# A hybrid decoder step on one core: the finish of a head pair is dealt out over all but the last four steps of the next pair's preparation

## The reference

```
for l in range(DEPTH):
    x = layer_norm(DN_ALPHA * x + 0.5 * swiglu(x, ffn1_w_in[l], ffn1_w_out[l]), ln1_g[l], ln1_b[l])
    proj = x @ w_in[l]
    f_r, f_s, f_g = jnp.split(proj, [R_PROJ, R_PROJ + S_PROJ], axis=-1)
    y_r, ... = rwkv7_mixer(f_r, ...)       # 4 heads x 64
    y_s, ... = swa_prompt(q, k, v, ...)    # window attention
    y_g, ... = gdn_mixer(f_g, ...)         # 4 heads x 64, chunked gated delta rule
    mix = jnp.concatenate([y_r, y_s, y_g], axis=-1) @ w_out[l]
    x = layer_norm(DN_ALPHA * x + mix, ln2_g[l], ln2_b[l])
    x = layer_norm(DN_ALPHA * x + 0.5 * swiglu(x, ffn2_w_in[l], ffn2_w_out[l]), ln3_g[l], ln3_b[l])
```

## Time and profile before

| | |
|---|---|
| median of 3 runs | 3004.49 us (2995.5 to 3006.26) |
| the profiled execution | 3005.59 us, of it the span from first to last instruction 3003.8 us |
| TensorE busy in matmuls | 2742.8 us, 91% of the span |
| TensorE busy in weight loads | 2561.6 us, 85% |
| VectorE busy | 1669.7 us, 56% |
| ScalarE busy | 949.2 us, 32% |
| chain that ended last | TensorE 78%, VectorE 10%, issue 5%, ScalarE 4% |
| mean granted TensorE clock | 0.901 of full speed |

### The profile page before, as it was taken

How to read it: one execution, slowest core, us unless ns; L and a number is a source line. 1 busy time by engine, 2 the same in 40 slices (tenths; PEclk the granted TensorE clock), 3 DMA queues, 4 the chain that set the end, 5 groups by cost and what they waited for, 6 DMA issues and landing times.

```text
span 3003.8 us, 59208 instructions
## 1 busy us (share of the span) xinstructions
PE 2742.8 (91%) x23222; PEld 2561.6 (85%) x23222; DVE 1669.7 (56%) x2503; ACT 949.2 (32%) x1694; POOL 161.5 (5%) x168
## 2 busy tenths in 40 slices
PE   8999999978796989999999999998887778999997
PEld 8999998866675889999999999987765668999996
DVE  5666347745545466664366653566445553666534
ACT  4333233322212243332233332344212222433323
POOL 1030110000000010001100001000000000100011
PEclk9999999976766999999999999998766768999998
DMA  4852234100000323232223222431000012222221
GB/s 110 101 93 86 85 107 121 44 27 1 9 9 1 91 66 90 85 89 83 86 78 88 87 85 85 129 90 41 7 1 8 9 28 86 77 84 84 87 87 59
DMA packets 380501, 201.67 MB, mean 67 GB/s; under 512 B 41461, under 2 KB 376821, under 8 KB 379528
## 3 DMA queue, kind: packets, MB, share of 16 engines
q1 hardware_dynamic: 377928, 197.46, 22.8%
q0 software_dynamic: 2400, 1.82, 1.9%
HBM read 188.07 MB, written 13.34 MB: 67 GB/s over the span
## 4 chain that ended last, share of the span: by engine, by line
PE 78%; DVE 10%; issue 5%; ACT 4%; DMA 1%; SPq 1%; DVEq 0%; POOLq 0%; ACTq 0%; POOL 0%
PE ps L682 51%; PE ps L737 25%; DVE ar L1918 3%; DVE ar L1912 2%; ACT ar L1415 2%; DVE wl L1796 1%; ACT wh L1346 1%; SPq L529 1%; PE ps L1011 1%; DVE x L1912 1%; DMA raws<-in_ffn_w_in 0%; DVE xl L1903 0%; DVE ar L1948 0%; ACT xh L1415 0%; DMA raws<-in_w_in 0%
## 5 line engine op out<-in xcount | busy, mean ns | idle before, releaser
L1796 DVE TENSOR_TENSOR wl<-raws,wh 128x1024 fp32r<-128x1024 f32 x336 | 411.3, 1225 | 673.1 <-ACT wh L1346 668.7
L737 PE MATMUL ps<-ar 64*64 64x64 f32 (+13 forms) x5408 | 517.6, 292 | 146.3 <-ACT ar L1415 39.0
L682 PE MATMUL ps<-xh,wh 128*128 128x272 f32 x2880 | 604.8, 291 | 17.7 <-DVE wl L1796 15.2
L737 PEld LDWEIGHTS ps<-ar 64*64 64x64 f32 (+6 forms) x5408 | 388.7, 177 | 250.2 <-issue 71.8
L682 PE MATMUL ps<-xh,wl 128*128 128x272 f32 x2880 | 599.7, 290 | 0.0
L682 PE MATMUL ps<-xl,wh 128*128 128x272 f32 x2880 | 598.3, 289 | 0.0
L1346 ACT ACTIVATE wh<-raws 128x1024 fp32r<-128x1024 f32 x336 | 354.7, 1057 | 416.6 <-PE ps L682 376.6
L682 PEld LDWEIGHTS ps<-xh,wh 128*128 128x128 f32 x2880 | 457.6, 190 | 21.4 <-DVE wl L1796 17.9
L682 PEld LDWEIGHTS ps<-xl,wh 128*128 128x128 f32 x2880 | 457.8, 190 | 0.0
L682 PEld LDWEIGHTS ps<-xh,wl 128*128 128x128 f32 x2880 | 457.3, 190 | 0.0
L682 PE MATMUL ps<-hh,wh 128*128 128x272 f32 x1408 | 292.3, 289 | 0.0
(11 more groups left out here) (188 smaller groups left out, 2749.9 us busy)
## 6 DMA issues: line engine op xcount, KB each, us to landing
raws<-in_ffn_w_in SPq DMA_DIRECT2D x176, 512.0 KB, 3.7
raws<-in_ffn_w_out SPq DMA_DIRECT2D x64, 512.0 KB, 4.0
raws<-in_w_in SPq DMA_DIRECT2D x42, 512.0 KB, 3.7
raws<-in_ffn_w_out SPq DMA_DIRECT2D x32, 384.0 KB, 3.4
raws<-in_w_out SPq DMA_DIRECT2D x16, 448.0 KB, 4.0
x_kept<-x SPq DMA_DIRECT2D x2, 2176.0 KB, 10.1
x<-x_kept SPq DMA_DIRECT2D x2, 2176.0 KB, 7.9
ar<-in_consts SPq DMA_DIRECT2D x2, 1337.5 KB, 6.7
```

The lines of the kernel that those rows point to most:

```text
L682: ins = pe.matmul(ps[:, bank + h, 0:n1 - h * NH], w[u % 2][:, k, :], a[:, k0 + k, h * NH:n1], start=(first and k == 0 and n == 0), stop=(l ...
L737: return pe.matmul(dst, lhsT, rhs, start=start, stop=stop, **kw)
L1796: dve.tensor_tensor(wl[u % 2][:, :, :], raw[u % 2][:, :, :], wh[u % 2][:, :, :].bitcast(F32), ALU.subtract).then_inc(sem("wl_done"), 1)
```

## The change

A fifth argument of `alternate`, `left`, is the number of steps at the end of the first generator beside which no step of the second stands. The keys of the second are multiplied by (n_first - left) / n_first. In the three rounds `left` is 4; the other two calls keep 0. Every instruction of before is there, with its waits; only the order changes, on each engine alike.

```diff
+NORM_AHEAD = 4
...
-def alternate(first, n_first, second, n_second):
+def alternate(first, n_first, second, n_second, left=0):

-    order = sorted([((k + 1) / n_first, 0) for k in range(n_first)] + [((k + 1) / n_second, 1) for k in range(n_second)])
+    share = (n_first - left) / n_first
+    order = sorted([((k + 1) / n_first, 0) for k in range(n_first)] + [((k + 1) / n_second * share, 1) for k in range(n_second)])
...
     for q in range(3):
-        alternate(prepare(q + 1), PREPARE_STEPS[q + 1], finish(q), FINISH_STEPS)
+        alternate(prepare(q + 1), PREPARE_STEPS[q + 1], finish(q), FINISH_STEPS, NORM_AHEAD)
```

## The result

The changed kernel took 3050.98 us in the median (3047.52 to 3060.32, 4 runs) beside 3005.38 for the kernel before (2995.5 to 3008.21): a ratio of 1.0163, with a 95% interval from 1.013 to 1.0195. The forecast was 3017, the top of the range 3038. The profiled execution took 3049.99 us, its span 3048.2, which is 44.4 more than before.

The account below looks back on a forecast made before the run. TensorE is at nine tenths outside the mixers, so only the rounds can change. Ends -13.6, stalls +16.0, front +4.9 and start -1.6 give +5.7 us a layer, +11.4 for both: from 3005.6 to 3017.0, range 2994 to 3038.

Parts of the forecast that it names:

- The ends: Ends of the three rounds: TensorE's two waits for `ge` (5.3 us each) and 3.0 into the mix saved; -13.6 a layer.
- The inner stalls: Inside the inverses: masks wait for newton (1.9 us) and F22 (3.4, gated pair 2.6), F20 0.45; +16.0 a layer.
- The start of the inverse in round 0: Before round 0's inverse: products of F15 and F16 move into TensorE's 3.83 us wait for VectorE; -1.6 us a layer.
- The clock for the norm: Half clock in inner stalls against faster first products of rounds 1 and 2: even, 0; ends -5 and +8 a layer.
- The front: Front of rounds 1 and 2: F6 before P8 makes VectorE wait, +2.7 and +2.2 us; +4.9 a layer.
- Clearly slower: Rival: the clock falls in four to six inner stalls a layer, 2.2 us each; 3025 to 3033, say 3030; 25%.
- Even: Rival: the rounds are bound by TensorE's total work, delays are absorbed and stalls take what the ends give; 3005; 21%.
- faster: Rival: end gaps close, clock holds over first products, inner stalls half covered, front free; -12.2 us a layer, 2981; 14%.
- The watch on the granted clock: Sign: the sum is wrong if the rounds' granted clock, 0.64 in round 1, moves by more than 0.03.

Follow-up runs that it names:

- The early `ge`: Kernel before, order kept; VectorE only makes the gates' copy `ge` for the next pair ahead of F22 instead of behind it: 2981.71 us, ratio 0.9947.
- F6 put back: Changed kernel with recurrence step F6 back behind P8 in rounds 1 and 2: 3046.01 us, ratio 1.0156 to the kernel before.
- The norm alone: Kernel before with only F19 to F22 moved ahead, not quite to the change's places; F1 to F18 as before: 3012.69 us, ratio 1.0037.
- the front alone: Kernel before with F1 to F18 where the change puts them and F19 to F22 as before: 3032.93 us, ratio 1.0103.
- the fillers: Changed kernel plus products leaving no result, three ahead of B of level 4, four ahead of level 5, all rounds: 3025.48 us, ratio 1.0085.
- the control: Kernel before with the same extra products at the same places, where TensorE doesn't wait: 3018.87 us, ratio 1.0044.
- recurrence-only kernel: Kernel before with only F1 to F12 where the change puts them, F13 to F22 as before: 3025.10 us, ratio 1.0078.

## Why the prediction was wrong

*The ends, -13.6.* Right: 5.3 at `ge` (5.85 to 0.56), and into the mix the first product comes 2.3 us behind the side copies, which end at 1016.6, where at most 3 was said.

*The inner stalls, +16.0.* Right in place and size: 2.38 for 1.9 and 3.38 for 3.4 in round 0, 2.38 and 3.60 in round 1, 1.98 and 2.56 (for 2.6) in round 2. Ends and stalls together come to +0.6 us of idle time in the three inverses of the first layer (21.4 for 20.8), for the +2.4 of these two terms.

*The start of the inverse in round 0, -1.6.* Wrong, and small. The moved products did not fill the wait that stands there; it grew from 3.83 to 5.06 us:

```profile
743.38 1.97 PE L739 MATMUL ps<-keep,ar 64*64 64x64 f32 x32 [5.06 <-DVE ar L1914]
```

*The clock for the norm, 0.* Right where the norm moves alone, and by the kind of balance that was given: the busy time of the stretch is 240.97 for 240.99. What the stalls lose in the inverses (6.5 us, for 4.4 forecast) comes back in the stretches behind them (6.5, for 5), most of it in round 1: 41.53 us of matmuls for 46.73. The early `ge`, which removes only the wait, shows the same there, 39.58. Beside a moved front, and in the change's own places, it isn't right; that comes below.

*The front, +4.9 with F6 as its cause.* The wait at F6 came as forecast, 3.67 for 3.7, and F6 put back took 5.0 and 6.8 us off rounds 1 and 2. But that is not the whole of the front: F1 to F18 alone cost 12.6 and 16.2 us a layer for the forecast's 4.9 less 1.6. The idle part of it, 5.4 and 5.1, is 2 us above that sum; in the change the stretches ahead of the inverses stand idle 7.1 us longer, for 3.3. That all idle time came out at +7.7 and +7.2 for +5.7 is in part luck: the front had more of it than forecast and the ends and stalls less. The other part, 7.2 and 11.1, is clock.

*The failed step* is the sentence that put the clock at 0 "with -5 and +8 a layer as ends". It counted only gaps inside and behind the inverse, where the norm went, and put nothing for F1 to F18. The whole term came out at +12.8 and +16.3, beyond the end of +8, and in rounds 1 and 2 alone at +14.3 and +14.1. More than half of this is there when only the recurrence, F1 to F12, moves: +7.8 in both layers. The norm alone has -2.7 in these rounds and the front alone +9.4, so 7.6 of the 14.3 are in neither. They come where the norm of the change has a second wait, ahead of B of level 4, and the fillers in these waits give back 8 us more than in the control. That this is the same 7.6 is argued from the size: no run has the norm in the places of the change without the front.

*The rivals.* "Clearly slower" had the right kind of cause and the nearest time, 3030, but put it in the stalls alone. "Even" is refuted by the interval, "faster" by the stalls, of which nothing was hidden.

*The watch on the granted clock* was well chosen, if it is read round by round. The text said that the sum would be wrong if the clock of the rounds moved by more than 0.03. In round 1 it went from 0.64 to 0.62, in round 2 with the start of the mix from 0.69 to 0.60. Over the whole stretch it hardly shows (0.67 to 0.65, since round 0 went up from 0.69 to 0.73 in the first layer); TensorE's busy time at equal counts shows it best.

*Slips in the working.* A front from 0 to 8 spans 3007 to 3023 by its own terms and not 3009 to 3026. Behind the idle end of round 0 the clock was still 0.50 to 0.58 up to 800.4 and not only to 800.2. Neither changes the forecast.

The Trainium skill (TensorE: Matmul & The Clock Gate, What's actually happening) has the slow clock as the default that activity releases. The filled waits agree: 2.08 us for the 64 products in place of 3.57. The group of 104 products can't be read by that sentence alone: TensorE was busy without a gap through it in both orders, and it took 8.54 us in one and 11.22 in the other.

*What stays open:* why the clock is lower in the inverses when only the recurrence ahead of them has moved. The waits ahead of them changed (idle in front +2.5 us in round 1, from 15.8 to 18.4). But it isn't simply that TensorE enters the inverse at a lower clock: in round 0 its first 5 us are at 0.50 in both orders, and the next 5 are at 0.69 before and at 0.50 with the recurrence moved. No run filled the waits ahead of the inverse. Nor is it explained that the recurrence-only kernel runs the same stretch of round 0 in 49.9 us in one layer and in 57.0 in the other, or the changed kernel in 53.0 and 59.9.

## What to carry to other kernels

Before spreading a follow-up stage over another, look for the one instruction that the stage's end holds up, and move only that: one copy of 0.43 us moved ahead gave about 0.5%, moving 22 steps to let it through cost 1.6%. Where the engine that bounds the kernel runs at a clock that falls and rises, compare its busy time at equal instruction counts, stage by stage, and give every moved step a clock term, also where it opens no gap. Compare such windows in stages that repeat: rounds 1 and 2 agreed to 0.2 us between the layers, round 0 of the change only to 3.6. And give every probe that adds work its control: the fillers gave back some clock even in the kernel that had no wait for them to fill. When the predicted waits come out and the time doesn't, look for the missing term outside the waits.

## What the runs showed of the hardware

In the recurrence-only kernel the same 257 matmuls with the same 8 us of idle time took 41.6 us in one layer and 48.9 in the other of one execution, at a granted clock of 0.76 and 0.64: an order of instructions doesn't by itself fix the clock that they get. Behind a wait of 2.4 us in the changed kernel 64 products ran at nearly half clock throughout (0.54 over their 3.57 us; 2.08 us with three products of no result in the wait). And TensorE can be busy without a gap and stay at half clock, as in this window of the recurrence-only kernel:

```profile
769.92:774.92 5.00, 5.00 (x37) 2.26 (x35) 0.42 (x1) 0.75 (x2) 0.00 (x0) 0.50 0.00 0
```
